# Expert down projection in three fp32r passes: low weight parts over the raw ones, four slots, empty list entries skipped

## The chip, the cores and the metric

One core of one Trainium2 chip runs the whole kernel in one launch. The metric is device time in microseconds; lower is better. The profile comes from one execution, which is a different one from the timed runs.

## The reference, cut to what matters

One decoder layer over 2048 prompt tokens and 64 sample tokens (2112 in all), width 1024: an input modulation, a projection into two mixers, an output projection with a layer norm, then a mixture of 32 experts and a second layer norm. The change touches the experts. What they compute:

```python
xt = u.reshape(B * L, D)                      # 2112 rows of 1024
eid = grp[:, None] * 8 + top_i                # two experts of one group for each row
def expert_block(args):                       # 128 rows of one expert
    xblk, ex = args
    h = jax.nn.silu(xblk @ w_gate[ex]) * (xblk @ w_up[ex])   # 1024 -> 256
    return h @ w_down[ex]                                    # 256 -> 1024
y = jnp.einsum("tkd,tk->td", y_slot.reshape(T, 2, D), wts)
x = layer_norm(ALPHA * x + gate2 * y)
```

All of it is float32. Each of the 32 experts has a gate, an up and a down matrix of 1 MB.

## The kernel before

The kernel runs five phases one after the other, each a block of five engine programs: `modulation_phase`, `mixer_phase`, `output_phase` (output projection, first norm, router logits, most of the routing), `expert_phase` and `combine_phase` (sum of a row's two expert results, second norm).

**Routing.** For each row the output phase and the head of the expert phase scatter two list entries into a list in memory; every expert has a region of 17 x 128 entries in it. An entry is (row of the input, row of the result, weight, 0). The list is first filled: an entry without a token reads the zero row `NTOK` of `u2_scratch` and writes one of 128 spare rows behind the results. The fill pattern is made in `output_phase`: POOL writes `slot_i` and `fill` (L1335 to L1337), DVE turns them into spare row numbers (L1500, L1502) in its turn of tile 0, and POOL sends the list after tile 1 (L1363).

**Blocks.** The expert phase works through blocks of 128 list entries, `total` of them, each expert with at least one and the total made even. PE runs `block_step(g, half)`: first half of `gate_up` of block g+1, transposes of the hidden rows of block g (L1908) and of the gathered rows of block g+2 (L1875), second half of `gate_up` (L1886, 24 matmuls of 512 columns in all, three fp32r passes over high and low parts), then the down projection of block g (L1925): four fp32 matmuls of 512 columns, which the trace shows as eight.

**Split of the weights.** `w_gate` and `w_up` land in `gu_raw`, three slots (`RAW`). ACT copies half a slot (128 x 2048) to the fp32r tile `gu_hi` (L1536, `split_high`), DVE subtracts it from the raw half into `gu_lo` (L1543, `split_low`); `gu_hi` and `gu_lo` have two slots. The down weights `dn_w` are used raw.

**Order on ACT and DVE.** Both run `expert_loop`: for each expert e the blocks before its last, `block_work(g, None)`, then `split_gu(e + 2, 0)`, the first half of the weights two experts on, then `block_work(last, e + 2)`, which has the second half inside it. For experts 30 and 31 nothing is split. ACT's `block_work(g)`: copy of the hidden transposes `hhT` (L1751), high part of block g+2 (`x_hi`, L1742), sigmoid of block g+1 (L1746), perhaps the second half split, and last the wait for the down projection of g and the copy `y_sb` with the weight (L1758). DVE's: low part `x_lo` (L1790), gate products `gsil`, `hh` (L1795, L1797), perhaps the second half split.

**Loads.** SP loads three experts ahead of everything, then in a loop `gate_up(e)`, which waits until expert e-3 is split, and `down(e - 1)`, which waits until the down projections up to expert e-4 are done. Every load waits for the landing of the one before it. POOL gathers the rows of block g+4 (L1684) and scatters the result of block g (L1718) by indirect transfers.

The order that matters below, as it stands in `expert_loop`:

```python
if gu_next is not None:
    split_gu(gu_next, 0, last)
block_work(last, gu_next)
```

Of the kernel before, what the change touches and what calls it, by code (L numbers as in the profile page):

```python
# [13 lines left out]

# [7 lines left out]
P = 128  # L22
D = 1024
KT = D // P
# [4 lines left out]
NTOK = SEQ + NSAMP  # L29
# [1117 lines left out]
def output_phase(nc, io, keep, scr):  # L1147
# [4 lines left out]
    T = TILES  # L1152
    LAST = T - 1
    with ExitStack() as ctx:
# [24 lines left out]
        slot_i = wo_raw[:, 6, 0:NLIST].bitcast(I32)  # L1179
# [16 lines left out]
        consts, fill_pre, fill_rdy, init_out, list_out = sem("consts2"), sem("fill_pre"), sem("fill_rdy"), sem("init_out"), sem("list_out")  # L1196
# [10 lines left out]
        with nc.Block() as block:  # L1207
# [108 lines left out]
            def _(pool):  # L1316
                pool.memset(u2[0:1, 1, :], 0.0)
# [14 lines left out]
                pool.wait_ge(consts, 1)  # L1332
                pool.dma_start(scr["u2"][NTOK:NTOK + 1, :], u2[0:1, 1, :]).then_inc(init_out, 16)
# [4 lines left out]
                pool.drain().then_inc(fill_pre, 1)  # L1338

                def tile(t):  # L1340
# [10 lines left out]
                    if t == 1:  # L1351
                        pool.wait_ge(init_out, 16)
# [90 lines left out]
            def _(dve):  # L1443
# [48 lines left out]
                for t in range(T):  # L1492
# [46 lines left out]
def split_low(dve, keep, e, a, s, r):  # L1539

    lo, hi = a * KT * DE, (a + 1) * KT * DE
    dve.wait_ge(keep["gu_h"], 2 * e + (a + 1))
    dve.tensor_tensor(w_slot(keep["gu_lo"], s, lo, hi), w_slot(keep["gu_raw"], r, lo, hi),  # L1543
                      w_slot(keep["gu_hi"], s, lo, hi).bitcast(F32), ALU.subtract).then_inc(keep["gu_l"], 1)
# [8 lines left out]
def expert_phase(nc, io, keep, scr):  # L1553
# [10 lines left out]
    gu_hi, gu_lo, dn_w, gu_l = keep["gu_hi"], keep["gu_lo"], keep["dn_w"], keep["gu_l"]  # L1564
# [7 lines left out]
    with ExitStack() as ctx:  # L1572
# [9 lines left out]
        hhT = sb("hhT", [P, KD, P])  # L1582
        y_sb = sb("y_sb", [P, 2, D])
# [25 lines left out]
        hT, hT_sb = sem("hT_ps"), sem("hT_sb")  # L1609
        dn, y_rdy, cur = sem("dn_done"), sem("y_rdy"), sem("cur_rdy")  # L1610
        kept = sem("kept")
# [8 lines left out]
        def expert_loop(eng, split_gu, block_work):  # L1620


            def expert(e, gu_next):
# [13 lines left out]
        with nc.Block() as block:  # L1637
            @block.sync
            def _(sp):
                def gate_up(e, s):  # L1640
                    if not (isinstance(e, int) and e < RAW):
                        wait_apart(sp, gu_l, 2 * (e - RAW) + 2, tick)
# [23 lines left out]
                gate_up(3, 0)  # L1666
                with sp.Fori(4, NE) as e:
                    gate_up(e, sp.snap(e % RAW))
                    down(e - 1, sp.snap((e - 1) % RAW))
                down(NE - 1, (NE - 1) % RAW)  # L1670

            @block.gpsimd
            def _(pool):
# [7 lines left out]
                def gather(b, at_ring, half):  # L1681
# [8 lines left out]
                pool.wait_ge(sc_out, 16 * 2 * (T - 12))  # L1690
                pool.dma_start(ids_ring[:, 0, :], scr["list"][0:P, :]).then_inc(ids_in, 16)
# [13 lines left out]
                def block(g, half):  # L1705
# [12 lines left out]
                    pool.indirect_dma_start(scr["y2"], bass.IndirectOffsetOnAxis(ap=ids_cur[:, half, 1:2], axis=0), y_sb[:, half, :], None).then_inc(y_out, 16)  # L1718
# [11 lines left out]
            def _(act):  # L1730
# [8 lines left out]

                def x_evac(b, half):  # L1740
# [584 lines left out]
```

## Time and profile before

| what | us |
|---|---|
| three runs | 1929.07, 1932.70, 1926.23 |
| median of the runs | 1929.07 |
| time of the profiled execution | 1924.06 |
| its span, first to last instruction | 1922.5 |
| first to last down projection, from the first start to the last | 1300.70 to 1793.99 |
| share of the span in which PE, DVE, ACT, POOL are busy | 91%, 60%, 32%, 30% |

The profile lists the busy time of each engine, its instructions in order of time with the idle time before them and what ended it, and a table of windows with the granted clock of TensorE (1.00 is 2.4 GHz). PEld is the weight load of PE. The timed runs lie up to 8.6 us above the profiled one, with a median 5.0 us above it.

### The profile page before, as it was taken

How to read it: one execution, taken by the hardware profiler on the slowest of the kernel's cores; microseconds unless marked ns; L12 is line 12 of the kernel's file. 1: busy time of each engine (PE TensorE's matmuls, PEld its weight loads, DVE VectorE, ACT ScalarE, POOL GpSimd, SP SyncE). 2: the span in 40 equal slices, each digit the busy share in tenths (PEclk: the TensorE clock that was granted, in tenths of full speed). 3: DMA queues.
4: the chain of work that ended last, by engine and by line, in shares of the span. 5: the costliest groups of instructions: out<-in, count | busy, mean ns of one | idle time of the engine just before them, and what ended most of it. 6: DMA issues, size and time to landing. Idle time of an engine off the chain costs nothing. (4 is left out here: it accounts for less than half of the span.)

```text
span 1922.5 us, 29621 instructions
## 1 busy us (share of the span) xinstructions
PE 1758.6 (91%) x9156; PEld 1378.1 (72%) x9157; DVE 1146.3 (60%) x1864; ACT 618.9 (32%) x770; POOL 586.1 (30%) x685
## 2 busy tenths in 40 slices
PE   5999999999999999999699999439999999999675
PEld 2888788888888899999577878326776677767321
DVE  3566655566666665666366877744466333455298
ACT  2333322233333322222131111025465434455233
POOL 0122221122222221122025466533344333334155
PEclk7999999999999999999899999659999999999897
DMA  8544344444333223332275443278899874798595
GB/s 258 151 133 123 96 140 133 118 125 138 89 105 93 84 61 89 94 101 68 71 247 193 132 132 121 93 263 284 301 353 379 299 238 167 250 322 313 202 397 177
DMA packets 301930, 342.76 MB, mean 178 GB/s; under 512 B 18932, under 2 KB 257300, under 8 KB 299391
## 3 DMA queue, kind: packets, MB, share of 16 engines
q1 hardware_dynamic: 278726, 284.30, 45.9%
q0 software_dynamic: 18000, 55.87, 7.9%
q10 hardware_dynamic: 5106, 1.31, 0.4%
q8 instruction: 57, 0.93, 0.2%
q14 instruction: 41, 0.34, 0.1%
HBM read 276.86 MB, written 64.58 MB: 178 GB/s over the span
## 5 line engine op out<-in xcount | busy, mean ns | idle before, releaser
L1543 DVE TENSOR_TENSOR w_gu_lo<-w_gu_raw,w_gu_hi (+1 forms) x64 | 146.5, 2292 | 133.3 <-ACT w_gu_hi L1536 121.8
L896 DVE TENSOR_TENSOR w_lo<-w_raw,w_hi 128x1024 fp32r<-128x1024 f32 x112 | 138.1, 1236 | 139.3 <-ACT w_hi L546 136.6
L658 POOL TENSOR_TENSOR o_r<-o_ms,neg_half 128x4 f32<-128x4 f32 (+1 forms) x16 | 16.8, 1050 | 663.1 <-DVEq L932 663.1
L713 PE MATMUL pr<-ub_hi,w_hi 128*128 128x288 f32 (+1 forms) x672 | 189.2, 335 | 0.0
L1886 PE MATMUL ph<-w_gu_hi,x_hi 128*128 (+1 forms) x408 | 183.5, 450 | 2.5 <-DVE x_lo L1790 2.5
L713 PE MATMUL pr<-ub_hi,w_lo 128*128 128x288 f32 (+1 forms) x672 | 184.2, 328 | 0.0
L713 PE MATMUL pr<-ub_lo,w_hi 128*128 128x288 f32 (+1 forms) x672 | 183.6, 327 | 0.0
L713 PE MATMUL pr<-ua_hi,w_hi 128*128 128x512 f32 x448 | 182.7, 408 | 0.0
L1925 PE MATMUL py<-w_dn_w,hhT 128*128 x400 | 179.9, 592 | 2.1 <-ACT hhT L1751 2.1
L713 PE MATMUL pr<-ua_lo,w_hi 128*128 128x512 f32 x448 | 177.0, 395 | 0.0
L713 PE MATMUL pr<-ua_hi,w_lo 128*128 128x512 f32 x448 | 177.0, 395 | 0.0
L1886 PE MATMUL ph<-w_gu_hi,x_lo 128*128 (+1 forms) x408 | 160.2, 393 | 0.0
L1886 PE MATMUL ph<-w_gu_lo,x_hi 128*128 (+1 forms) x408 | 160.0, 392 | 0.0
L546 ACT ACTIVATE w_hi<-w_raw 128x1024 fp32r<-128x1024 f32 x112 | 118.0, 1054 | 51.7 <-PE pr L713 42.5
L1790 DVE TENSOR_TENSOR x_lo<-pxe,x_hi 128x1024 f32 (+1 forms) x52 | 63.5, 1220 | 117.6 <-ACT x_hi L1742 117.6
L1536 ACT ACTIVATE w_gu_hi<-w_gu_raw (+1 forms) x64 | 121.9, 1907 | 34.1 <-DMA w_gu_raw<-in_w_e_up 18.7
L1925 PEld LDWEIGHTS py<-w_dn_w,hhT 128*128 128x128 f32 x400 | 75.5, 189 | 78.5 <-issue 74.8
L713 PEld LDWEIGHTS pr<-ub_hi,w_hi 128*128 128x128 f32 x672 | 113.3, 188 | 18.0 <-issue 9.0
L1718 POOL DMA_INDIRECT y_scratch<-y_sb,ids_cur x50 | 51.6, 1031 | 239.4 <-ACT y_sb L1758 210.2
L713 PEld LDWEIGHTS pr<-ub_hi,w_lo 128*128 128x128 f32 x672 | 113.4, 188 | 10.2
L713 PEld LDWEIGHTS pr<-ub_lo,w_hi 128*128 128x128 f32 x672 | 113.7, 188 | 8.8
L670 POOL TENSOR_TENSOR kl<-kl,wl 128x256 f32<-128x256 f32 (+1 forms) x112 | 89.0, 795 | 95.0 <-DVEq L1035 77.8
(337 smaller groups left out, 3502.1 us busy)
## 6 DMA issues: line engine op xcount, KB each, us to landing
w_raw<-in_w_in SPq DMA_DIRECT2D x112, 512.0 KB, 4.2
w_gu_raw<-in_w_e_gate SPq DMA_DIRECT2D x32, 1024.0 KB
w_gu_raw<-in_w_e_up SPq DMA_DIRECT2D x32, 1024.0 KB
w_dn_w<-in_w_e_down SPq DMA_DIRECT2D x32, 1024.0 KB
w_mod<-in_w_mod SPq DMA_DIRECT2D x16, 1024.0 KB
y_t<-y_scratch SPq DMA_DIRECT2D x16, 1024.0 KB, 7.6
w_ring<-in_w_mod SPq DMA_DIRECT2D x4, 2048.0 KB, 17.5
x_cols<-in_x_prompt SPq DMA_DIRECT2D x32, 256.0 KB, 5.4
```

Source lines behind the costliest of these rows:

```text
L546: act.activation(w_hi[:, n % WS], w_raw[:, n % WRAW], ACT.Copy).then_inc(hi_done, 1)
L658: pool.tensor_tensor(o_r[:, 0:c], o_ms[:, 0:c], keep["neg_half"][:, 0:c], ALU.pow).then_inc(o_rs, 1)
L670: pool.tensor_tensor(dst[:, :, 0, :], src[:, :, 0, :], wr, ALU.mult)
L713: last = pe.matmul(pr[n % 2][:, a * 512:a * 512 + c], w[:, n % WS, k, :], x[:, k, a * c:(a + 1) * c], start=(k == 0 and m == 0), stop=(k = ...
L896: dve.tensor_tensor(w_lo[:, n % WS], w_raw[:, n % WRAW], w_hi[:, n % WS].bitcast(F32), ALU.subtract).then_inc(lo_done, 1)
L1536: act.activation(w_slot(keep["gu_hi"], s, lo, hi), w_slot(keep["gu_raw"], r, lo, hi), ACT.Copy).then_inc(keep["gu_h"], 1)
L1543: dve.tensor_tensor(w_slot(keep["gu_lo"], s, lo, hi), w_slot(keep["gu_raw"], r, lo, hi), w_slot(keep["gu_hi"], s, lo, hi).bitcast(F32), AL ...
L1718: pool.indirect_dma_start(scr["y2"], bass.IndirectOffsetOnAxis(ap=ids_cur[:, half, 1:2], axis=0), y_sb[:, half, :], None).then_inc(y_out, 16)
L1790: dve.tensor_tensor(x_lo[:, bass.ds(half, 1), :].rearrange("p a w -> p (a w)"), px[:, :], x_hi[:, bass.ds(half, 1), :].rearrange("p a w -> ...
L1886: last = pe.matmul(ph[:, half, :], x[:, half, k * P:(k + 1) * P], w_slot(w, s, k * GU, (k + 1) * GU), start=(k == 0 and m == 0), stop=(k = ...
L1925: last = pe.matmul(py[:, hf * 512:(hf + 1) * 512], hhT[:, k, :], w_slot(dn_w, s_down, at, at + 512), start=(k == 0), stop=(k == KD - 1))
```

## The change

In the expert phase:

- The down weights are split like the others: ACT writes `dn_hi` (two slots), DVE the low part. `expert_loop` gets `split_dn(e + 1)` behind the last block of expert e, on ACT and on DVE. The hidden rows are split as well: ACT's copy becomes `hT_hi`, and DVE's `block_work` begins with the low part `hT_lo`. PE does twelve fp32r matmuls of 512 columns for a down projection, and waits for `hT_l` and `dn_l` in place of `hT_sb` and `wd_in`.
- `gu_lo` and `dn_lo` lie over the raw slots, and there are four slots instead of three. A gate and up load of expert e now waits until the gate-up matmuls of all blocks up to expert e-4 are done, where it waited for the split of e-3; `down(e)` stands directly behind `gate_up(e)`.
- `y_sb` and the small routing tiles share one tile, `board`.

In the routing: an entry without a token now holds the row number `NO_ROW` twice, which lies beyond both bounds; the gather and the scatter skip it. POOL clears `xg` once. The zero row, the spare rows, `slot_i` and DVE's two instructions on it are gone.

```diff
-RAW = 3
+RAW = 4
+NO_ROW = 2 * NTOK
@@ output_phase, POOL and DVE
-                pool.iota(slot_i[:, :], pattern=[[1, NLIST]], base=0, channel_multiplier=NLIST)
-                pool.iota(fill[:, :, 0], pattern=[[0, NLIST]], base=NTOK, channel_multiplier=0)
+                pool.iota(fill[:, :, 0:2], pattern=[[0, NLIST], [0, 2]], base=NO_ROW, channel_multiplier=0)
                 pool.memset(fill[:, :, 2:4], 0)
-                    if t == 0:
-                        dve.wait_ge(fill_pre, 1)
-                        dve.tensor_scalar(slot_i[:, :], slot_i[:, :], P - 1, None, ALU.bitwise_and)
-                        dve.drain()
-                        dve.tensor_scalar(fill[:, :, 1], slot_i[:, :], 2 * NTOK, None, ALU.add)
-                        dve.drain().then_inc(fill_rdy, 1)
@@ helpers
+def split_down_high(act, keep, e, s, r):
+    act.wait_ge(keep["wd_in"], 16 * e + 16)
+    act.activation(w_slot(keep["dn_hi"], s, 0, DE // P * D), w_slot(keep["dn_w"], r, 0, DE // P * D), ACT.Copy).then_inc(keep["dn_h"], 1)
+
+def split_down_low(dve, keep, e, s, r):
+    dve.wait_ge(keep["dn_h"], e + 1)
+    dve.tensor_tensor(w_slot(keep["dn_lo"], r, 0, DE // P * D), w_slot(keep["dn_w"], r, 0, DE // P * D), w_slot(keep["dn_hi"], s, 0, DE // P * D).bitcast(F32), ALU.subtract).then_inc(keep["dn_l"], 1)
@@ expert_loop
                 block_work(last, gu_next)
+                if not (isinstance(e, int) and e == NE - 1):
+                    split_dn(e + 1)
@@ SP
-                        wait_apart(sp, gu_l, 2 * (e - RAW) + 2, tick)
+                        wait_apart(sp, gu, blocks_before(sp, e - (RAW - 1)), tick)
@@ POOL, gather and scatter
-                                            bass.IndirectOffsetOnAxis(ap=ids_now[:, 0:1], axis=0)).then_inc(xg_in, 16)
+                                            bass.IndirectOffsetOnAxis(ap=ids_now[:, 0:1], axis=0),
+                                            bounds_check=NTOK - 1, oob_is_err=False).then_inc(xg_in, 16)
+                pool.memset(xg[:, :, :], 0.0).then_inc(cleared, 1)
@@ ACT and DVE, block_work
-                    act.activation(hhT[:, :, :], pht[:, 0:KD * P].rearrange("p (k t) -> p k t", k=KD), ACT.Copy).then_inc(hT_sb, 1)
+                    act.activation(hT_hi[:, :, :], pht[:, 0:KD * P].rearrange("p (k t) -> p k t", k=KD), ACT.Copy).then_inc(hT_h, 1)
+                    dve.wait_ge(hT_h, g + 1)
+                    dve.tensor_tensor(hT_lo[:, :, :], pht[:, 0:KD * P].rearrange("p (k t) -> p k t", k=KD),
+                                      hT_hi[:, :, :].bitcast(F32), ALU.subtract).then_inc(hT_l, 1)
                     x_evac(g + 2, dve.snap(g % 2))
@@ PE, block_step
-                    pe.wait_ge(hT_sb, g + 1)
-                    pe.wait_ge(wd_in, 16 * e_now + 16)
+                    pe.wait_ge(hT_l, g + 1)
+                    pe.wait_ge(dn_l, e_now + 1)
                     pe.wait_ge(y_rdy, g + 1)
-                            last = pe.matmul(py[:, hf * 512:(hf + 1) * 512], hhT[:, k, :], w_slot(dn_w, s_down, at, at + 512),
-                                             start=(k == 0), stop=(k == KD - 1))
+                            for m, (x, w) in enumerate(((hT_hi, hi), (hT_hi, lo), (hT_lo, hi))):
+                                last = pe.matmul(py[:, hf * 512:(hf + 1) * 512], x[:, k, :], w,
+                                                 start=(k == 0 and m == 0), stop=(k == KD - 1 and m == 2))
```

## Rows read from the trace of the kernel before

**Rows 1.** The page, part 1: busy us (share of the span) and instructions.

```profile
PE 1758.6 (91%) x9156; PEld 1378.1 (72%) x9157; DVE 1146.3 (60%) x1864; ACT 618.9 (32%) x770; POOL 586.1 (30%) x685
```

**Rows 2.** Windows (start:end, length, busy us by engine, PEclk, DMA share, GB/s), expert phase.

```profile
1300.70:1794.00 493.30, 491.22 (x2060) 346.22 (x2059) 234.52 (x208) 247.25 (x256) 186.34 (x248) 1.00 0.82 286
1400.83:1470.90 70.07, 70.07 (x295) 49.48 (x294) 45.31 (x36) 44.83 (x42) 29.99 (x35) 1.00 1.06 380
```

**Rows 3.** Timeline of PE (start, us, line, operation, count [idle before]), one block.

```profile
1400.83 3.59 PE L1925 MATMUL py<-w_dn_w,hhT 128*128 x8
1403.86 0.79 PE L1886 MATMUL ph<-w_gu_hi,x_hi 128*128 x1
1404.49 0.40 PE L1886 MATMUL ph<-w_gu_lo,x_hi 128*128 x1
1404.72 0.39 PE L1886 MATMUL ph<-w_gu_hi,x_lo 128*128 x1
...
1410.84 3.59 PE L1925 MATMUL py<-w_dn_w,hhT 128*128 x8
```

**Rows 4.** Timeline of ACT and DVE, a one-block expert.

```profile
1404.59 1.12 ACT L1758 ACTIVATE y_sb<-py,ids_cur 128x1024 f32 x1 [1.24 <-PE py L1925]
1406.74 1.91 ACT L1536 ACTIVATE w_gu_hi<-w_gu_raw  x1 [1.03 <-issue]
1409.02 2.29 DVE L1543 TENSOR_TENSOR w_gu_lo<-w_gu_raw,w_gu_hi  x1 [3.11 <-ACT w_gu_hi L1536]
1411.23 1.22 DVE L1790 TENSOR_TENSOR x_lo<-pxe,x_hi 128x1024 f32 x1
...
1412.36 0.41 DVE L1795 TENSOR_TENSOR gsil<-ph,gsig 128x256 f32<-128x256 f32 x1
```

**Rows 5.** Timeline of ACT, a last block behind another of its expert.

```profile
1334.51 1.12 ACT L1758 ACTIVATE y_sb<-py,ids_cur 128x1024 f32 x1 [3.05 <-PE py L1925]
1335.52 1.90 ACT L1536 ACTIVATE w_gu_hi<-w_gu_raw  x1
```

**Rows 6.** Timeline of ACT: first splits of one-block experts, first and last of 19.

```profile
1316.65 1.92 ACT L1536 ACTIVATE w_gu_hi<-w_gu_raw  x1 [1.05 <-issue]
...
1759.83 1.91 ACT L1536 ACTIVATE w_gu_hi<-w_gu_raw  x1 [1.01 <-DMA w_gu_raw<-in_w_e_up]
```

**Rows 7.** Timeline of ACT and PE where the hidden rows came late.

```profile
1481.42 0.36 ACT L1751 ACTIVATE hhT<-pht 128x256 f32<-128x256 f32 x1
...
1482.18 3.69 PE L1925 MATMUL py<-w_dn_w,hhT 128*128 x8 [1.08 <-ACT hhT L1751]
```

**Rows 8.** Timeline, output phase, tiles 0 and 1.

```profile
993.92 2.99 DVE L1447 TENSOR_TENSOR y_lo<-y_raw,y_hi 128x1024 fp32r<-128x1024 f32 x1 [0.57 <-ACT y_hi L1270]
...
997.00 2.46 DVE L1500 TENSOR_SCALAR wo_raw<-wo_raw 128x561 int32<-128x561 int32 x1
...
1000.36 1.23 DVE L1459 TENSOR_TENSOR z<-pm,mod_p 128x1024 f32<-128x1024 f32 x1
...
1014.51 1.97 PE L1390 MATMUL px<-ident,u 128*128 128x128 f32 x8 [3.78 <-POOL u L1357]
```

**Rows 9.** Timeline of PE, combine phase: two tiles behind a wait.

```profile
1847.72 5.37 PE L2054 MATMUL ps_y<-y_t,ident 128*128 128x512 f32 x8 [1.98 <-DVE zw L2063]
...
1859.43 3.67 PE L2054 MATMUL ps_y<-y_t,ident 128*128 128x512 f32 x8 [2.38 <-DVE zw L2063]
```

**Rows 10.** Windows (columns of Rows 2), the first of these tiles.

```profile
1847.70:1852.70 5.00, 4.98 (x8) 2.02 (x8) 4.70 (x8) 1.58 (x3) 2.44 (x4) 0.66 1.02 420
```

**Rows 11.** Timeline of POOL, start of the expert phase.

```profile
1283.72 1.00 POOL L1684 DMA_INDIRECT xg<-u_scratch,ids_now  x1 [0.80 <-POOL ids_now L1682]
...
1288.05 0.19 POOL L1682 COPY ids_now<-ids_ring 128x4 int32<-128x4 int32 x1 [2.23 <-DMA xg<-u_scratch,ids_now]
```

**Rows 12.** Timeline, end of the expert phase.

```profile
1799.85 1.01 POOL L1718 DMA_INDIRECT y_scratch<-y_sb,ids_cur  x1 [5.88 <-ACT y_sb L1758]
...
1807.85 0.35 SPq L1975 DMA_DIRECT2D y_t<-y_scratch  x1
```

More of the change, by code:

```diff
@@ L1563, in expert_phase @@
     ident, blk_tab, exp_tab = keep["ident"], keep["blk_tab"], keep["exp_tab"]
-    gu_hi, gu_lo, dn_w, gu_l = keep["gu_hi"], keep["gu_lo"], keep["dn_w"], keep["gu_l"]
+    gu_hi, gu_lo, dn_hi, dn_lo, gu_l, dn_l = (keep[n] for n in ("gu_hi", "gu_lo", "dn_hi", "dn_lo", "gu_l", "dn_l"))
     wg_in, wu_in, wd_in = keep["wg_in"], keep["wu_in"], keep["wd_in"]
@@ L1581, in expert_phase @@
         hh = sb("hh", [P, DE])
-        hhT = sb("hhT", [P, KD, P])
-        y_sb = sb("y_sb", [P, 2, D])
+        hT_hi = sb("hT_hi", [P, KD, P], F32R)
+        hT_lo = sb("hT_lo", [P, KD, P], F32R)
+        y_sb = R["board"][:, :].rearrange("p (a d) -> p a d", a=2)
         ids_ring = sb("ids_ring", [P, RING, 4], I32)
@@ L1618, in blocks_before, with expert_loop @@
             return eng.value_load(exp_tab[0:1, bass.ds(e, 1)], min_val=0, max_val=MAXB)
-        def expert_loop(eng, split_gu, block_work):
+        def expert_loop(eng, split_gu, split_dn, block_work):
             def expert(e, gu_next):
@@ L1665, in _ @@
                 sp.wait_ge(xg_in, 32)
[L1666 to L1670, printed above, removed]
+                with sp.Fori(RAW, NE) as e:
+                    s = sp.snap(e % RAW)
+                    gate_up(e, s)
+                    down(e, s)
             @block.gpsimd
@@ L1717, in block @@
                         wait_apart(pool, y_out, 16 * g, tick)
-                    pool.indirect_dma_start(scr["y2"], bass.IndirectOffsetOnAxis(ap=ids_cur[:, half, 1:2], axis=0), y_sb[:, half, :], None).then_inc(y_out, 16)
+                    pool.indirect_dma_start(scr["y2"], bass.IndirectOffsetOnAxis(ap=ids_cur[:, half, 1:2], axis=0), y_sb[:, half, :], None,
+                                            bounds_check=NO_ROW - 1, oob_is_err=False).then_inc(y_out, 16)
                 block(0, 0)
@@ L1738, in split_gu, with split_dn @@
                     split_high(act, keep, e, a, act.snap(e % 2), act.snap(e % RAW))
+                def split_dn(e):
+                    split_down_high(act, keep, e, act.snap(e % 2), act.snap(e % RAW))
                 def x_evac(b, half):
@@ L1779, in _ @@
                 act.wait_ge(tab_sb, 1)
-                expert_loop(act, split_gu, block_work)
+                expert_loop(act, split_gu, split_dn, block_work)
             @block.vector
@@ L1786, in split_gu, with split_dn @@
                     split_low(dve, keep, e, a, dve.snap(e % 2), dve.snap(e % RAW))
+                def split_dn(e):
+                    split_down_low(dve, keep, e, dve.snap(e % 2), dve.snap(e % RAW))
                 def x_evac(b, half):
@@ L1862, in _ @@
                 dve.wait_ge(tab_sb, 1)
-                expert_loop(dve, split_gu, block_work)
+                expert_loop(dve, split_gu, split_dn, block_work)
             @block.tensor
@@ L1884, in gate_up @@
                             pe.wait_ge(gu_l, 2 * e + 2)
-                        for m, (x, w) in enumerate(((x_hi, gu_hi), (x_hi, gu_lo), (x_lo, gu_hi))):
-                            last = pe.matmul(ph[:, half, :], x[:, half, k * P:(k + 1) * P], w_slot(w, s, k * GU, (k + 1) * GU),
+                        hi = w_slot(gu_hi, s, k * GU, (k + 1) * GU)
+                        lo = w_slot(gu_lo, r, k * GU, (k + 1) * GU)
+                        for m, (x, w) in enumerate(((x_hi, hi), (x_hi, lo), (x_lo, hi))):
+                            last = pe.matmul(ph[:, half, :], x[:, half, k * P:(k + 1) * P], w,
                                              start=(k == 0 and m == 0), stop=(k == KT - 1 and m == 2))
@@ L1900, in _ @@
                 transposes(0, 0)
-                gate_up(0, 0, 0, 0, lambda: transposes(1, 1))
+                gate_up(0, 0, 0, 0, 0, lambda: transposes(1, 1))
                 pe.wait_ge(tab_sb, 1)
@@ L1917, in between @@
                         transposes(g + 2, half)
-                    gate_up(g + 1, e_next, s_next, 1 - half, between)
-                    pe.wait_ge(hT_sb, g + 1)
-                    pe.wait_ge(wd_in, 16 * e_now + 16)
+                    gate_up(g + 1, e_next, s_next, r_next, 1 - half, between)
+                    pe.wait_ge(hT_l, g + 1)
+                    pe.wait_ge(dn_l, e_now + 1)
                     pe.wait_ge(y_rdy, g + 1)
@@ L2300, in build, with weights @@
         with ExitStack() as ectx:
-            for name, slots, width, dt in (("gu_raw", RAW, 2 * KT * DE, F32), ("gu_hi", 2, 2 * KT * DE, F32R),
-                                           ("gu_lo", 2, 2 * KT * DE, F32R), ("dn_w", RAW, DE // P * D, F32)):
-                keep[name] = ectx.enter_context(nc.sbuf_tensor("w_" + name, [P, slots, width], dt))
-            for name in ("wg_in", "wu_in", "wd_in", "gu_h", "gu_l"):
+            def weights(stack, name, slots, width, dt):
+                keep[name] = stack.enter_context(nc.sbuf_tensor("w_" + name, [P, slots, width], dt))
+            GUW, DNW = 2 * KT * DE, DE // P * D
+            with ExitStack() as landing:
+                weights(landing, "gu_raw", RAW, GUW, F32)
+                weights(landing, "dn_w", RAW, DNW, F32)
+            weights(ectx, "gu_lo", RAW, GUW, F32R)
+            weights(ectx, "dn_lo", RAW, DNW, F32R)
+            weights(ectx, "gu_hi", 2, GUW, F32R)
+            weights(ectx, "dn_hi", 2, DNW, F32R)
+            for name in ("wg_in", "wu_in", "wd_in", "gu_h", "gu_l", "dn_h", "dn_l"):
                 keep[name] = ectx.enter_context(nc.semaphore(name))
```

67 lines of the change are left out of this document (39 added, 28 removed).

## Prediction

> **What bounds the kernel now.** I read the page's busy times first: PE is busy in 91% of the span, and DVE, the engine that gets most of the new work, in 60% [rows 1]. These shares are means over five phases, so I cut the expert phase out with the windows. From the first to the last down projection it is 493.3 us, PE is busy in 491.2 of them at a granted clock of 1.00, DVE in 234.5, ACT in 247.3 [rows 2]. The timeline of PE shows a block: the eight fp32 records of one down projection start at 1400.83, those of the next at 1410.84, with no idle time between: 10.01 us a block, and 49 of these make 490.5 [rows 3]. The 2.8 us left over lie in two or three waits in the middle. So PE bounds all 50 blocks, and less PE work pays as long as nobody else is late. The rest of the argument is whether somebody becomes late.
>
> **PE, per block.** The down projection takes from 1400.83 to 1403.86, and the first fp32r matmul behind it needs 0.63 where the ones after it follow at 0.23 [rows 3]. I take both together: 3.66 us from the start of the fp32 records to the second fp32r matmul. With the change these are 13 fp32r matmuls of 512 columns. Their pace is 0.228 us (23 of them and the transposes fill 1404.49 to 1410.84 [rows 3]), so 2.96 us. PE wins 0.70 us a block: 10.01 becomes **9.31 us**, if nothing else is late. Over 49 steps that is 34 us.
>
> **ACT and DVE: the new ring.** Added are one copy of 128 x 2048 on ACT and one subtraction of that size on DVE for each expert, and one subtraction of 128 x 256 on DVE for each block. Their durations have rows: 1.91 and 2.29 us (the halves of gate and up have the same size), and 0.41 us for a 128 x 256 operation from PSUM [rows 4]. In sum DVE gets 32 x 2.29 + 50 x 0.41 = 94 us on top of 234.5, and stays under 70% of the stretch. By busy time it fits. By order it need not: `split_dn(e + 1)` stands behind ACT's wait for the down projection of the last block of e; `split_gu(e + 3, 0)` of the next expert stands behind that; and on DVE the new `hT_lo`, for which PE now waits, stands behind both of their low parts. When expert e+1 has only one block, all this lies between two down projections. I add it up, from the start of one down projection (0):
>
> - `y_sb` starts when the matmuls are done. The last of twelve starts at 2.51 and takes 0.39; `y_sb` started 0.17 behind the end of the old ones (1400.83 + 3.59 to 1404.59) [rows 3, 4], so 3.07, and 3.12 because a first record behind a wait is up to 0.1 longer (3.69 for 3.59) [rows 3, 7].
> - `split_dn` on ACT follows `y_sb` at 1.01 after its start, as the split does in a two-block expert [rows 5]: 4.13 to 6.04.
> - The low part on DVE starts some 0.3 later (0.37 from 1408.65 to 1409.02) [rows 4]: 6.34.
> - The low part of `split_gu` comes right behind it. Its high part on ACT is done by 6.04 + 1.91 = 7.95, before DVE is free, so it costs nothing; two subtractions follow each other at 2.21 (1409.02 to 1411.23) [rows 4]: 8.55, and `hT_lo` starts at 10.76 and ends at 11.17.
> - PE starts 0.40 behind the operation it waits for (1481.78 to 1482.18) [rows 7]: **11.6 us**.
>
> That is 1.6 us more than the 10.01 of now, and PE, done in 9.3, waits 2.3 us in each. What hides behind what: ACT's control work between `y_sb` and the next split shows now as 1.03 us of idle time behind a `y_sb` of 1.12 [rows 4]. I price it at nothing, because 1.9 us of new ACT work covers it; if that fails, the first split ends at 8.98 instead of 7.95 and the ring takes 12.4 us.
>
> The Trainium skill bears on this ("Advanced Engine Details and Errata", Sequencer and Instruction Queues): the sequencer goes on reading while its engine works, and ACT and DVE have queues of eight. By that rule the control work is covered and the ring takes 11.6; without it, 12.4. No row here shows ACT with two long operations queued before a loop's end, so the run will tell.
>
> **Where an expert has more blocks.** Before its first block only the down split is in the way: 6.34 + 2.21 + 0.41 + 0.40 = 9.36. Before its last block only `split_gu` is: 3.12 + 1.01 [rows 5] + 1.91 + 0.37 + 2.21 + 0.41 + 0.40 = 9.43. Blocks between these have neither. So these steps stay near PE's 9.31; I take 9.36.
>
> **How many of each.** In the timeline the first split of a one-block expert comes 1.0 us behind the end of `y_sb`, that of a longer one with it. I count 19 one-block experts with this pattern [rows 6] and 11 longer ones; the two last experts have no split of gate and up. The steps are then 19 x 11.6 + 30 x 9.36 = 220.4 + 280.8 = 501.2 us against 493.3: **+7.9 us**. The gain of PE (30 x 0.65 = 19.5, and the 2.8 of waits) is less than what the ring takes (19 x 1.6 = 30.2).
>
> **The clock.** A wait of 2.3 us is new to this stretch, whose clock is 1.00 throughout [rows 2]. The combine phase has waits of this size on PE: of eight tiles behind waits of 1.96 to 2.38 us five took 5.37 us or more, and three took 3.67, with the same instructions [rows 9]; the granted clock of such a slow tile is 0.66 over 5 us, so it was at 1.2 GHz at first and rose to 2.4 [rows 10]. A fall costs 1.7 us, and the down projection that starts behind the wait is on the ring. Bounds: no fall, 0; a fall at each, 19 x 1.7 = 32. The expert phase works more densely than the combine phase, but the wait is as long, so I take half: **+16 us**.
>
> **Loads.** The loads for expert e now start when the gate-up of e-4 is done, some two steps before they are needed (23 us and more), and 3 MB take 8.3 us at the 380 GB/s of seven one-block steps, where DMA was full (share 1.06) [rows 2]. With steps of 11.6 us and the empty entries not moved, the demand falls from 380 to below 340 GB/s. I price them at 0; if they came late, each one-block step could lose 1.3, as the two late ones of now did.
>
> **At the start** the fourth expert's 3 MB are on the way when POOL gathers blocks 0 to 2. The gather of block 1 takes 4.3 us now [rows 11]; with weights beside it I allow 6 to 8, so between 0 and +4, and some of it has slack: **+1.6**. The added split of expert 0 and POOL's clearing of `xg` (128 x 2048) lie in idle time of DVE, ACT and POOL ahead of the first gather.
>
> **Output phase.** DVE's two instructions on the fill pattern stand between `y_lo` and the next tile's `z`: 996.91 to 1000.36. Without them everything behind `z` moves 3.3 us, up to the transposes for which PE waits 3.78 us [rows 8]. Behind them PE is busy nearly throughout, so it is kept: **-3.3**. POOL's longer fill is in its idle time.
>
> **At the end** the last scatter is issued at 1799.85, and the combine phase begins 8 us later [rows 12]. If most entries of the last block are empty, up to 3 us go: **-1**. Elsewhere skipped entries shorten only transfers that nobody waits for: 0.
>
> **Sum:** +7.9 + 16 + 1.6 - 3.3 - 1 = +21. The profiled execution would go from 1924.06 to 1945. The median of the runs lies 5.0 above the profiled one, so I add 21 to 1929.07: **1950 us**. A difference of 0.3% (5.8 us) is about what a measurement can tell from none.
>
> **Rivals.**
>
> 1. *The ring without the clock.* The clock stays at 1.00, as it does at the two waits of 1.0 to 1.1 us in this phase [rows 7]. Then +21 - 16 = +5: 1934. Against it: the waits are twice as long, and [rows 9]. Chance 0.2.
> 2. *The ring, longer.* Falls at nearly each wait, or control work that is not covered (19 x 0.8 = 15): +21 + 16 to + 31, around 1970 and up to 1981. Chance 0.17.
> 3. *PE bounds as before* (the other side). It needs DVE ready within 9.3 us in the one-block steps: that the two low parts (4.4 us) don't both lie between `y_sb` and `hT_lo`, say because ACT gets ahead of the down projection it waits for. Then 49 x 9.31 = 456.2, so -37, and with start, end and output phase -40: 1889. It decides from a ring of 9.3; for any gain at all the ring must stay under 10.9. Speaking for it: the busy sums alone (DVE 234.5 + 94 = 329, ACT 247.3 + 32 x 1.9 = 308, of 456). Against: the order of the two programs, each in order. Chance 0.13. The Trainium skill ("FP8 and Floating Point Precision", TensorE Precision Notes) says that true fp32 takes four passes through the array; three for four is the gain that this case would cash in full.
> 4. *Loads come late.* The gate of the loads is one expert later than it was, and DMA was full. All 19 one-block steps lose 1.3 more: +21 + 25, 1975. Chance 0.07.
>
> The forecast itself (ring, clock falls at a part of the waits, 1935 to 1966) has 0.43.
>
> **How the numbers follow.** Faster: rival 3, 0.13, and 0.01 for rival 1 with a larger gain in the output phase: 0.14. Within 0.3% (1923.3 to 1934.9): two thirds or more of rival 1 and the low end of the forecast: 0.18. Slower: 0.68. The range reaches from 1929, rival 1 with no cost at the start, to 1981, the end of rival 2; it leaves out rival 3 and little above.
>
> **What would show it.** Right: in the timeline of a one-block expert, down projections 11.6 us apart, with PE idle 2.3 us before each and DVE (`hT_lo`) named as what ended it; on DVE `dn_lo`, `gu_lo` and `hT_lo` back to back; 9.3 to 9.4 us elsewhere; the windows of one-block stretches with a clock between 0.8 and 1.0. Wrong: steps of 9.3 throughout (rival 3); PE waiting for ACT's first split (12.4); ACT waiting for DMA (rival 4); and `z` of tile 1 no earlier behind `y_lo`.

## The result, and the profile after

| | before | changed kernel |
|---|---|---|
| median of the runs, us | 1930.88 (4 runs) | 1987.93 (4 runs, 1984.39 to 1991.03) |
| ratio to before, 95% interval | | 1.0311 (1.0288 to 1.0334) |
| profiled execution, us (its span) | 1924.06 (1922.5) | 1990.59 (1987.7) |
| first to last down projection, us | 493.3 | 560.56 (1297.92 to 1858.48) |
| 19 steps at one-block experts, mean us | 10.14 | 13.84 |
| the 30 other steps, mean us | 10.02 | 9.92 |
| first start of `z` in tile 0 to that in tile 1, output phase | 14.50 | 11.12 |

PE is TensorE, DVE VectorE, ACT ScalarE and POOL GpSimd. A step is the time from the start of one down projection to the start of the next; a one-block step is one in which ACT and DVE do all the splits of a one-block expert's turn between the two. The change makes the kernel 3.1% slower. Between the first and the last down projection 67.3 us come in, and the span grows by 65.2, so the loss lies there. The one-block steps take 262.9 us in sum where they took 192.8 (+70.1); the others give back 2.8.

The page of the changed kernel, part 1 (as [rows 1]): PE is busy in 89%, where it was in 91%, and its busy time grew from 1758.6 although it has less to do.

```profile
PE 1767.3 (89%) x9356; PEld 1437.1 (72%) x9357; DVE 1238.0 (62%) x1944; ACT 674.6 (34%) x802; POOL 627.4 (32%) x683
```

Windows of it (columns of [rows 2]): ten one-block experts, then longer ones, then seven one-block experts.

```profile
1400.00:1540.00 140.00, 111.12 (x453) 88.06 (x452) 89.73 (x71) 79.79 (x70) 55.69 (x50) 0.86 0.82 272
1540.00:1700.00 160.00, 158.23 (x766) 129.47 (x765) 74.15 (x80) 75.91 (x81) 61.60 (x81) 0.99 0.57 187
1700.00:1810.00 110.00, 95.19 (x419) 76.08 (x418) 69.71 (x58) 64.53 (x60) 46.20 (x48) 0.92 0.74 243
```

In the first window PE idles 29 of 140 us at a granted clock of 0.86. In the middle one it is nearly as full as before. DMA moves 272 GB/s where the first seven of these experts took 380 before [rows 2].

The timeline of PE, one step (answers to [rows 3]):

```profile
1407.82 0.49 PE L1945 MATMUL py<-w_dn_hi,hT_hi 128*128 x1 [1.94 <-DVE hT_lo L1812]
...
1408.60 0.47 PE L1945 MATMUL py<-w_dn_hi,hT_hi 128*128 x1
1408.87 0.63 PE L1945 MATMUL py<-w_dn_lo,hT_hi 128*128 x1
...
1411.86 0.56 PE L1945 MATMUL py<-w_dn_hi,hT_lo 128*128 x1
1412.25 0.40 PE L1903 MATMUL ph<-w_gu_hi,x_hi 128*128 x1
...
1422.47 0.79 PE L1945 MATMUL py<-w_dn_hi,hT_hi 128*128 x1 [3.43 <-DVE hT_lo L1812]
```

And ACT and DVE in the same step (answers to [rows 4]):

```profile
1412.59 1.12 ACT L1765 ACTIVATE board<-py,ids_cur 128x1024 f32 x1 [4.36 <-PE py L1945]
1413.60 1.90 ACT L1537 ACTIVATE w_dn_hi<-w_dn_w  x1
1415.41 1.90 ACT L1525 ACTIVATE w_gu_hi<-w_gu_raw  x1
...
1415.84 2.29 DVE L1542 TENSOR_TENSOR w_dn_lo<-w_dn_w,w_dn_hi  x1 [4.14 <-ACT w_dn_hi L1537]
1419.46 2.29 DVE L1532 TENSOR_TENSOR w_gu_lo<-w_gu_raw,w_gu_hi  x1 [1.33 <-issue]
1421.67 0.42 DVE L1812 TENSOR_TENSOR hT_lo<-pht,hT_hi 128x256 fp32r<-128x256 f32 x1
```

Read together, these are the ring: down projection 1407.82, `y_sb` (now a part of `board`) 4.77 later, `dn_lo` 3.25 after that, `gu_lo` 3.62 after that, `hT_lo` 2.21 after that, the next down projection 0.80 later. In sum 14.65. The parts in their order are the predicted ones, and two have another size. `y_sb` comes late because eight of the twelve matmuls run at half the pace (0.43 us apart, 1.2 GHz) before PE is back at 0.23. The windows of this step show the clock: it is still 1.00 in the wait, and 0.50 from one microsecond behind the start of the burst.

```profile
1405.50:1407.80 2.30, 0.37 (x2) 0.00 (x0) 2.30 (x3) 1.75 (x2) 2.30 (x1) 1.00 1.05 363
1408.80:1412.20 3.40, 3.40 (x9) 2.64 (x8) 2.72 (x3) 0.00 (x0) 0.00 (x0) 0.50 0.65 218
```

And `gu_lo` doesn't follow `dn_lo` at once: DVE idles 1.33 us "<-issue", waiting for nothing that the profile shows.

The waits from 1290 to 1870 and, in the second fence, the page's group of the first matmul of each three: nearly all of PE's idle time is `hT_lo`. The third line is DVE's gap, once in each one-block step; the fourth is ACT's wait for POOL's copy of the slot numbers, which holds `y_sb` back in three blocks.

```profile
ACT board L1765 <- PE py L1945: 153.7, 47, 7.1
PE py L1945 <- DVE hT_lo L1812: 54.4, 20, 3.9
DVE w_gu_lo L1532 <- issue: 13.5, 19, 1.8
ACT board L1765 <- POOL ids_cur L1716: 8.2, 3, 2.7
```

```profile
L1945 PE MATMUL py<-w_dn_hi,hT_hi 128*128 x200 | 94.0, 470 | 55.2 <-DVE hT_lo L1812 54.4 <-issue 0.5
```

ACT has no wait for DMA in this stretch, so the loads are not late. In the output phase the gap that DVE's two fill instructions left is closed (answers to [rows 8]):

```profile
984.50 1.22 DVE L1454 TENSOR_TENSOR z<-pm,mod_p 128x1024 f32<-128x1024 f32 x1
...
992.45 3.08 DVE L1442 TENSOR_TENSOR y_lo<-y_raw,y_hi 128x1024 fp32r<-128x1024 f32 x1 [0.48 <-ACT y_hi L1271]
995.62 1.22 DVE L1454 TENSOR_TENSOR z<-pm,mod_p 128x1024 f32<-128x1024 f32 x1
...
1009.56 1.97 PE L1385 MATMUL px<-ident,u 128*128 128x128 f32 x8 [3.35 <-POOL u L1352]
```

### The profile page after: what moved, and what is told of

The parts are those of the page before. It is cut to its first block and busy times, and to the rows that moved or that the text cites. A ratio compares the mean times of both kernels' runs of the same rounds, so it can differ in the third digit from the quotient of the medians.

```text
span 1987.7 us, 30591 instructions
## 1 busy us (share of the span) xinstructions
PE 1767.3 (89%) x9356; PEld 1437.1 (72%) x9357; DVE 1238.0 (62%) x1944; ACT 674.6 (34%) x802; POOL 627.4 (32%) x683
## 5 line engine op out<-in xcount | busy, mean ns | idle before, releaser
L660 POOL TENSOR_TENSOR o_r<-o_ms,neg_half 128x4 f32<-128x4 f32 (+1 forms) x16 | 16.8, 1051 | 662.9 <-DVEq L934 662.9
L1903 PE MATMUL ph<-w_gu_hi,x_hi 128*128 (+1 forms) x408 | 167.4, 410 | 5.8 <-issue 3.4
L1945 PE MATMUL py<-w_dn_hi,hT_hi 128*128 x200 | 94.0, 470 | 55.2 <-DVE hT_lo L1812 54.4
L1542 DVE TENSOR_TENSOR w_dn_lo<-w_dn_w,w_dn_hi (+1 forms) x32 | 73.4, 2292 | 103.9 <-ACT w_dn_hi L1537 103.9
L1721 POOL DMA_INDIRECT y_scratch<-board,ids_cur x50 | 51.4, 1028 | 266.2 <-issue 261.6
L1765 ACT ACTIVATE board<-py,ids_cur 128x1024 f32 x50 | 55.9, 1117 | 161.9 <-PE py L1945 153.7
## 6 DMA issues: line engine op xcount, KB each, us to landing
w_gu_raw<-in_w_e_up SPq DMA_DIRECT2D x32, 1024.0 KB, 10.5
```

Source lines behind the costliest of these rows:

```text
L1542: dve.tensor_tensor(w_slot(keep["dn_lo"], r, 0, DE // P * D), w_slot(keep["dn_w"], r, 0, DE // P * D), w_slot(keep["dn_hi"], s, 0, DE // P ...
L1765: act.activation(y_sb[:, bass.ds(now, 1), :].rearrange("p a d -> p (a d)"), py[:, :], ACT.Copy, scale=ids_cur[:, bass.ds(now, 1), 2:3].rea ...
L1903: last = pe.matmul(ph[:, half, :], x[:, half, k * P:(k + 1) * P], w, start=(k == 0 and m == 0), stop=(k == KT - 1 and m == 2))
L1945: last = pe.matmul(py[:, hf * 512:(hf + 1) * 512], x[:, k, :], w, start=(k == 0 and m == 0), stop=(k == KD - 1 and m == 2))
```

## The experiments

Ten kernels ran. Each ratio is to runs of the kernel before taken beside it. "Falls" are the down projections behind the one-block steps, of 19, that ran partly at 1.2 GHz by the granted clock.

### One place of the ring at a time

**`hT_lo` first.** On DVE the first half of the next gate and up split goes behind `hT_lo` in the last block's work:

```diff
-                if gu_next is not None:
+                if gu_next is not None and not low_first:
                     split_gu(gu_next, 0, last)
@@ DVE, block_work, behind hT_lo
+                    if gu_next is not None:
+                        split_gu(gu_next, 0)
```

> The changed kernel with one thing moved: on DVE, in the last block of an expert, hT_lo comes ahead of the first low part of gate and up, no longer behind it. Nothing is left out. Theory (a ring of y_sb, split_dn on ACT, low part of down, low part of gate and up, hT_lo, down projection; PE then waits some 2.3 to 3 us and its clock falls): 2.2 us leave the ring of each of the 19 one-block steps, and with the wait under 1 us the clock stays up. These steps then take 9.8 to 10.4 us instead of 13.8, the whole some 65 to 75 us less than the changed kernel: 1915 to 1925. Rival a (twelve fp32r matmuls and their weight tiles are slow by themselves, or memory placement is): steps stay above 12, 1970 or more. Rival b (the loads come too late with the new gate): no change either, since the order on DVE doesn't touch loads: 1980 to 1990.

Measured: 1922.51, ratio 0.9966 (0.9951 to 0.9981); 495.5 us from first to last down projection, one-block steps 10.73, others 9.72. With `gu_lo` and the gap ahead of it no longer between `y_sb` and `hT_lo`, 65 us are gone. The one-block step is still above PE's 9.31 and above the 9.8 to 10.4 expected, and the clock did not stay up throughout: in five of these steps PE waits 2.35 to 2.64 us, and behind four of them the clock fell. What is left shows in the waits of the same stretch:

```profile
ACT board L1765 <- POOL ids_cur L1716: 30.0, 13, 3.7
PE py L1947 <- DVE hT_lo L1812: 16.0, 8, 2.6
```

ACT's `y_sb` now waits for POOL's copy of the slot numbers in 13 blocks, where the changed kernel had three such waits (8.2 us). Here POOL's copy and ACT behind it:

```profile
1423.27 2.36 POOL L1716 COPY ids_cur<-ids_ring 128x4 int32 x1
...
1434.86 0.20 POOL L1716 COPY ids_cur<-ids_ring 128x4 int32 x1
```

```profile
1425.85 1.12 ACT L1765 ACTIVATE board<-py,ids_cur 128x1024 f32 x1 [3.38 <-POOL ids_cur L1716]
```

**Down split early.** On ACT and DVE `split_dn(e + 1)` moves into the last block's work, on ACT ahead of the wait for the down projection:

```diff
-                block_work(last, gu_next)
-                if not (isinstance(e, int) and e == NE - 1):
-                    split_dn(e + 1)
+                block_work(last, gu_next, None if isinstance(e, int) and e == NE - 1 else e + 1)
@@ ACT and DVE, block_work, behind the second half of split_gu
+                    if dn_next is not None:
+                        split_dn(dn_next)
```

> The changed kernel with split_dn(e + 1) moved, on ACT and on DVE, into the last block of expert e, ahead of ACT's wait for the down projection. Nothing is left out. Theory of the ring: the down split leaves it; what stays is y_sb at 3.1, 2.15 of control, 1.9 high part, 0.4, 2.2 low part, 0.4 hT_lo, 0.4 = 10.6 us for a one-block step, PE waits some 1.3 us, and the clock falls rarely: 1925 to 1945. Rival a (slow down projection): above 1970. Rival b (loads): the down weights are needed some 2 us earlier, so waits for DMA appear on ACT: 1990 or more.

Measured: 1917.60, ratio 0.9948 (0.9929 to 0.9966); 487.9 us, one-block steps 10.62, others 9.54. The step is what the parts give with the down split taken out (10.6 expected); the time lies below the 1925 to 1945 that was expected. PE still waits for `hT_lo` at 20 places, 0.5 to 1.1 us each, and the window of the one-block experts has the full clock:

```profile
PE py L1947 <- DVE hT_lo L1812: 15.1, 20, 1.1
```

```profile
1400.00:1540.00 140.00, 131.69 (x631) 105.97 (x630) 100.37 (x87) 92.05 (x85) 66.16 (x70) 1.00 0.88 303
```

**Both moves** together, the two diffs above:

> Both moves of the two runs before in one kernel. Theory of the ring: the chain from y_sb to hT_lo no longer has a low part in it (3.1 + 2.15 + 1.9 + 0.4 + 0.4 + 0.4 = 8.4 us), so PE bounds at 9.3 us or ACT at 9.5; 49 x 9.5 = 466 us against 493 before: 1900, faster than both kernels by 1% or more. If loads or the down projection itself cost the time, it stays above 1960.

Measured: 1903.38, ratio 0.9882 (0.9859 to 0.9904); 469.2 us, one-block steps 9.92, others 9.36. Of the 49 steps 36 now take the 9.31 that PE needs. So PE's gain is real where the ring leaves it, and the order on ACT and DVE had hidden it.

### The rest of the change alone

The down projection stays fp32, without the split of `w_dn` and `hT_lo`; slots, waits of the loads, skipped entries and the fill are the change's:

```diff
-                    pe.wait_ge(hT_l, g + 1)
-                    pe.wait_ge(dn_l, e_now + 1)
+                    pe.wait_ge(hT_h, g + 1)
+                    pe.wait_ge(wd_in, 16 * e_now + 16)
```

> The changed kernel with the down projection taken back to four fp32 matmuls on raw weights: no down split, no hT_lo. Four slots, low parts over raw ones, the new gate of the loads, skipped entries and the shared tile stay. Theory of the ring: the chain is as before the change, y_sb, split, hidden copy, under 9 us, so PE bounds at 10.0: the kernel before less what the output phase gains, 1922 to 1930. If the four slots, the gate of the loads or the skipped entries cost the time, it stays above 1960.

Measured: 1923.44, ratio 0.9980 (0.9965 to 0.9995); 495.3 us, 10.22 and 10.04 a step. Less than 0.3% and no loss: all of the 3.1% belongs to the three passes and what feeds them.

**The fill alone**, in the kernel before: DVE's two instructions are gone, and all entries without a token write one spare row.

```diff
-                pool.iota(slot_i[:, :], pattern=[[1, NLIST]], base=0, channel_multiplier=NLIST)
+                pool.iota(fill[:, :, 1], pattern=[[0, NLIST]], base=2 * NTOK, channel_multiplier=0)
```

> The kernel before with one edit in the output phase: the spare row of an entry without a token is a constant that POOL writes, and DVE's two instructions on it are gone. Nothing is left out of the result; all such entries write one spare row. Theory: z of tile 1 starts 3.3 us earlier and this is kept, 1.5 to 4 us less than the kernel before. Rival: other work is late next and takes it up, 0 to 1 us; or writes to one row are slow and cost time at the end of the expert phase.

Measured: 1930.55, ratio 1.0010 (0.9991 to 1.0029). `z` to `z` went from 14.50 to 11.16, as in the changed kernel, but the total is unmoved: the 1.5 to 4 us expected did not come. In this profile the 16th to the 19th step took 11.1 to 13.0, where the splits came late because of late loads, and first to last down projection was 498.9. So the 3.3 us are shown where they arise, and whether they reach the end is not.

### The clock

Spare 128-column fp32 matmuls ahead of PE's wait for `hT_lo` in each block of the changed kernel keep PE occupied in a part of that wait; their result goes nowhere. Eight of them, then four:

```diff
+                    for _ in range(8):
+                        pe.matmul(rk[:, 0:P], keep["ones"][:, :], keep["tri"][:, :], start=True, stop=True)
                     pe.wait_ge(hT_l, g + 1)
```

> The changed kernel with eight added 128-column fp32 matmuls on PE ahead of its wait for hT_lo in every block, into a free bank that nobody reads (1.7 us of work). Nothing is left out. Theory of the clock: in one-block steps they fit into a wait of 2.3 to 3 us, the wait that is left is about 1 us, the down projection behind it runs at 2.4 GHz, and y_sb starts 3.1 instead of 4.8 us behind its start; one-block steps go from 13.8 to 12.2 to 12.6, while the others go from 9.9 to 11.0. In sum within 10 us of the changed kernel. Rival (the slow down projections come from something else, such as weight tiles or memory placement): y_sb stays 4.8 behind, one-block steps stay at 13.8, and the whole is 30 us longer.

> The changed kernel with four spare 128-column fp32 matmuls in place of the eight of the run that kept the clock, again ahead of TensorE's wait for hT_lo in each block; their result goes nowhere. They take about 0.85 us at the full clock instead of 1.7, so that at one-block experts a wait of 1 to 3 us is left. Theory A (the falls of the clock come from TensorE's waits of 2 to 4 us): some of the 19 down projections behind the waits still run partly at 1.2 GHz, more than the 2 of 19 with eight matmuls and fewer than the 18 of 19 with none; down to y_sb at one-block experts lies between 3.2 and 4.8 on average; the other 30 steps pay 0.85 less than with eight, about 10.5; the time is 1985 to 2000. Rival B (the falls do not depend on how long TensorE waits): 15 or more of 19 still fall and the time is 2010 to 2020, the changed kernel's plus 0.6 to 0.85 for most blocks.

| | changed kernel | four | eight |
|---|---|---|---|
| median, ratio to before | 1987.93, 1.0311 | 1985.50, 1.0302 (1.0276 to 1.0327) | 2005.81, 1.0405 (1.0377 to 1.0433) |
| waits of PE in one-block steps, us | 1.9 to 3.9 | 1.3 to 2.7 | 0.2 to 2.0 |
| falls, of 19 | 18 | 5 | 2 |
| down projection to `y_sb`, mean us | 4.55 | 3.51 | 3.34 |
| one-block step, mean us | 13.84 | 12.86 | 12.83 |
| other step, mean us | 9.92 | 10.36 | 11.19 |

The first window of the three kernels has a granted clock of 0.86, 0.96 and 0.98. With eight:

```profile
1425.79 1.95 PE L1937 MATMUL rk_last<-tri,ones 128*128 128x128 f32 x16
1429.39 0.50 PE L1947 MATMUL py<-w_dn_hi,hT_hi 128*128 x1 [1.65 <-DVE hT_lo L1812]
```

PE got 0.9 (four) and 1.8 us (eight) more to do in each block, and the one-block steps still became 1.0 shorter. `y_sb` comes 1.0 and 1.2 us earlier. That is the price of the falls, and the waits cause them: shorter waits, fewer falls. With eight the one-block step (12.83 for 12.2 to 12.6) and the total (18 us above the changed kernel, for 10) missed what was expected: the 30 other steps pay 1.27 each, 38 us, where 1.1 was expected, and the one-block steps give back less than expected, because DVE's gap is no shorter (`gu_lo` 3.2 us behind `dn_lo` in the mean). With four the two sides cancel: no gain over the changed kernel.

### DVE's gap behind `dn_lo`

In the changed kernel `gu_lo` starts 2.49 to 4.06 us behind `dn_lo`, 3.00 in the mean, and 2.21 would be back to back. The lines between the two on DVE are the loop's turn to the next expert, the reading of its bounds and a branch. This run puts the low part of `w_dn` behind them, on DVE alone:

```diff
             def expert(e, gu_next):
                 first = blocks_before(eng, e)
                 last = eng.snap(eng.value_load(exp_tab[0:1, bass.ds(e + 1, 1)], min_val=1, max_val=MAXB) - 1)
+                if dn_first:
+                    split_dn(e)
@@
-                if not (isinstance(e, int) and e == NE - 1):
+                if not dn_first and not (isinstance(e, int) and e == NE - 1):
                     split_dn(e + 1)
@@ DVE, ahead of the loop
-                split_down_low(dve, keep, 0, 0, 0)
 ...
-                expert_loop(dve, split_gu, split_dn, block_work)
+                expert_loop(dve, split_gu, split_dn, block_work, dn_first=True)
```

> The changed kernel with one edit on VectorE alone: it reads the bounds of the next expert before it takes the low part of w_dn, so that this reading no longer stands between the ends of dn_lo and the start of gu_lo; what is computed is the same. In the changed kernel the start of gu_lo lies 2.98 us (mean) behind the start of dn_lo, of which 2.29 is dn_lo itself. Theory A (the gap of some 0.7 is VectorE's own reading of bounds, which the prediction priced at nothing): dn_lo to gu_lo falls to 2.2 to 2.5, the reading goes into VectorE's wait for ScalarE's w_dn_hi, the steps at one-block experts become 0.5 to 0.7 shorter (13.84 to 13.2), and the time falls by 10 to 13 us to about 1975 to 1978. Rival B (the gap is the rest of the loop's control, or the clash with GpSimd's copies): dn_lo to gu_lo stays at 2.8 to 3.0 and the time within 3 us of the changed kernel's 1988.

Measured: 1956.66, ratio 1.0162 (1.0140 to 1.0185); 520.35 us, one-block steps 11.91, others 9.80. DVE in one step:

```profile
1415.70 2.29 DVE L1542 TENSOR_TENSOR w_dn_lo<-w_dn_w,w_dn_hi  x1 [2.57 <-ACT w_dn_hi L1537]
1417.91 2.28 DVE L1532 TENSOR_TENSOR w_gu_lo<-w_gu_raw,w_gu_hi  x1
1420.11 0.42 DVE L1814 TENSOR_TENSOR hT_lo<-pht,hT_hi 128x256 fp32r<-128x256 f32 x1
```

and PE, the end of this step and that of a later one:

```profile
1420.94 0.51 PE L1946 MATMUL py<-w_dn_hi,hT_hi 128*128 x1 [2.08 <-DVE hT_lo L1814]
...
1491.08 0.79 PE L1946 MATMUL py<-w_dn_hi,hT_hi 128*128 x1 [2.06 <-DVE hT_lo L1814]
1491.67 0.63 PE L1946 MATMUL py<-w_dn_lo,hT_hi 128*128 x1
```

The gap is gone in all 19 (2.20 to 2.21), and sixteen of these steps take 11.56 to 11.73: the ring of 11.6 that was predicted. The gain is more than twice the expected one. The waits shrank to between 1.55 and 2.11 us in 18 of 19, and falls to 5, three of them in a row from the step that ends at 1491.08. So the sum for one-block steps is -36.5 us: 19 x 0.79 = 15.0 for the gap, and 19 x (4.55 - 3.41) = 21.7 for falls that no longer happen. The loop's turn and the reading of the bounds were moved as one; which of the two weighs more isn't told apart, nor why the gap varies between 0.2 and 1.8. The branch still stands between `dn_lo` and `gu_lo` here, and leaves no gap.

### The better versions

POOL's copy of the slot numbers at the top of its block's work, ahead of the list load and the gather:

```diff
+                    pool.tensor_copy(ids_cur[:, half, :], place(ids_ring, g % RING)).then_inc(cur, 1)
 ...
-                    pool.tensor_copy(ids_cur[:, half, :], place(ids_ring, g % RING)).then_inc(cur, 1)
```

With `hT_lo` first:

> The changed kernel with hT_lo ahead of the low part of the next expert's first gate and up weights on VectorE, as in the run at 1922.5, and GpSimd's copy of the slot numbers moved to the top of its block's work; the same is computed. In the run at 1922.5 ScalarE's y_sb waited 13 times on GpSimd's copy, 30.0 us in all, and the clock fell behind some of TensorE's waits. Theory A (those waits carry what is left above the run with both moves): one-block steps go from 10.73 to 9.9 to 10.2 and the time to 1903 to 1912. Rival B (the waits on GpSimd stand beside a wait for the split of w_dn that ends as late): the time stays at 1918 to 1923.

Measured: 1906.86, ratio 0.9897 (0.9877 to 0.9917); one-block steps 10.05 against 10.73, others 9.57. The waits of `y_sb` on POOL are gone, and with them every wait of PE above 1.4 us and every fall of the clock. With both moves:

> The kernel with both moves, and on POOL the copy ids_cur of block g at the top of its block, ahead of the fetch and the gather, no longer behind them. Nothing is left out. In the kernel with both moves some one-block steps still take 10 to 11 us, and there y_sb waits for that copy (2.4 us long beside DVE's work, 0.2 otherwise). Theory: y_sb then starts with the end of the down projection or of ACT's split, the steps of 10.0 to 11.0 fall to 9.3 to 9.6, 8 to 11 us less than with both moves alone. Rival: these steps come from ACT's or DVE's own control work; then nothing changes.

Measured: **1898.90, ratio 0.9852** (0.9821 to 0.9883), the fastest of all; 466.8 us, 9.80 and 9.35 a step. That is 4.5 us less than with both moves alone, where 8 to 11 were expected, and the two intervals overlap, so this last gain is not clear of noise. Its slow steps (10.5 to 11.2, from 1435 to 1490) now wait for weights, as the waits of that window show:

```profile
ACT w_gu_hi L1525 <- DMA w_gu_raw<-in_w_e_up: 14.3, 5, 3.2
```

## Why the prediction was right in its sign and wrong in its size

The forecast was 1950 with a range of 1929 to 1981; it came out at 1988. Against the sum of the prediction, in the profiled execution (+65.2 of span where +21 was summed):

| term | predicted | measured |
|---|---|---|
| ring without falls, 19 steps | 19 x 11.6 | 19 x 12.4 (the DVE gap, 0.79 each): **+15** |
| falls of the clock in it | 16 | 19 x (4.55 - 3.12) = 27.2, less the 1.7 of the next line, nearly all in the 14 one-block steps that begin with a fall: **+9.5** |
| `y_sb` held back by POOL's copy | 0 | 4.83 - 3.12 in the first one-block step, whose clock did not fall: **+1.7** |
| 30 other steps | 30 x 9.36 | 30 x 9.92: **+17** |
| down projection of the first block | +1.6 | 60.79 us from the start of the phase, against 59.70: +1.1 |
| output phase | -3.3 | `z` to `z` -3.4, and 2.5 of it is left at the expert phase's first load (3.9 earlier, of which 1.4 were there before tile 0): +0.8 |
| end | -1 | 129.2 us from the last down projection to the end, against 128.5: +0.7 |

1. **PE per block, 9.31: right.** Undisturbed steps take 9.30 to 9.34 in the changed kernel, and with both moves 36 of the 49 do.
2. **The ring's places and sizes: right but for one.** `y_sb` to `dn_lo` took 3.26 (3.22 summed), `gu_lo` to `hT_lo` 2.21, `hT_lo` to the down projection 0.80 (0.81 summed). The order on ACT and DVE is what costs, as the two moves show by taking it out one place at a time.
3. **The step that failed** is the sentence "The low part of `split_gu` comes right behind it". I had looked for control work on ACT, priced it there (0.8 us if not covered), and found none in the result: `gu_hi` follows `dn_hi` at 1.81 with no idle time. On DVE the same loop's turn stands between `dn_lo` and `gu_lo`, and I gave it no term. The subtraction's 2.29 us don't cover it. On ACT two operations cover the turn, `y_sb` and `dn_hi`: 2.82 us from the start of the first to `gu_hi`, against the 2.15 that the turn takes there. So the reading ahead on which the prediction relied hid all of it on ACT and only a part on DVE. The row that could have told stood in [rows 4]: ACT takes 2.15 us from the start of `y_sb` to its next split over the same lines of code, nearly as long as the 2.29 of cover on DVE. The Trainium skill ("Advanced Engine Details and Errata", Clock Domains) gives DVE's sequencer 0.96 GHz and the others 1.2; by that the 2.15 us would be an estimated 2.7 on DVE. Measured are 2.49 to 4.06 with a mean of 3.00, so the rule points the right way and explains neither end.
4. **The clock: right in kind, mis-sized.** "I take half" of 19 became 18. Of the 18, 14 lie at the start of one-block steps and 4 at the start of others (point 5). The half came from a combine phase whose waits were 1.96 to 2.38 us [rows 9], and there the last of the eight tiles counted has half the rows, so that it was four of seven with the same instructions; with the DVE gap the waits here grew to between 1.9 and 3.9. Where the ring had its predicted length, and the waits 1.55 to 2.11 but for one of 2.94, 5 of 19 fell: less than half. So this error is mostly a consequence of the one before. A fall does not make the wait behind it longer, since PE's own work grows with it: in the run without DVE's gap the waits behind two fallen projections were 2.07 and 2.11 us, where the others but one lie between 1.55 and 2.11.
5. **The other steps: mis-sized.** 9.36 held for the fastest; the mean was 9.92. Of the 17 us, 8.2 lie in four steps that begin with a fall (12.28, 11.06, 11.23, 11.06), and 2.4 in one of 11.81 whose clock stayed up: there ACT waited 2.74 us for POOL's copy and `y_sb` came at 5.27. I had let falls end with the one-block step, but the last one of a group falls on the first down projection of the next expert. The rest is mostly steps of 9.9 to 10.0 that alternate with 9.3; with both moves, where `hT_lo` comes earlier, all but two are gone. I read them as PE's own turn of its loop, which it can't read ahead when it reaches the wait for `hT_lo` only just in time; that reading is argued, not tested.
6. The errors add up to nearly what came out: 21.2 + 15.0 + 9.5 + 1.7 (POOL) + 16.8 + 0.8 (output phase) - 0.5 (start) + 1.7 (end) - 1.4 (by which the changed kernel's profile was ahead at tile 0 already) = 64.8, of 65.2. **Loads, start, output phase: right,** and small. No wait for a load stands in this stretch of the changed kernel; such waits came in versions with shorter steps, at 9.3 us and, with the fp32 down projection, at 10.0 (PE waits 2.8 us in sum for down weights). **End: wrong** by 1.7.

The rivals: the second (falls at nearly each wait, or control work) names falls and control work, with an "or" where the chip had "and". But its control work stood on ACT, where it was covered; that its 15 us met the 15.0 of DVE's gap is luck. Its end of 1981 is what both together give, and the other steps lie above it. The third, PE as the bound, is what the two moves restore. Its limit for any gain, a ring under 10.9, doesn't follow from the prediction's own sums: (493.3 - 280.8) / 19 is 11.2.

Had the DVE gap not been there, the forecast would have stood, in part by luck: the run without it is at a ratio of 1.0162, which is 1960 on the scale of the 1929.07. In its profile the 19 one-block steps with their falls take 226 us where 236 were summed, and the 30 others 294 where 281 were, so two misses of 10 and 13 us nearly cancel.

## What to carry to other kernels

Write the ring between two uses of the bounding engine as a list of starts, and put every loop turn and register read on every engine of it in as a term, also behind a wait, which did not absorb it here (DVE idled 4.14 us ahead of `dn_lo` and 1.33 behind it). When the ring comes out above the bounding engine's own work, the wait it makes can cost TensorE its clock, so price the ring and the falls together: 0.79 us taken out of this ring was worth 1.9 us a step. A precision trick that moves work from the busiest engine to idle ones pays (1.5% here) only after the new work is taken off the path behind the last result: split weights ahead of the wait, and serve the small operand first.

## What the runs showed of the hardware

- The granted clock falls at waits of about 2 us: 18 of 19 at waits of 1.9 to 3.9 us, 5 of 19 at 1.55 to 2.9, 5 of 19 at 1.3 to 2.7 (four spare matmuls), none at 0.5 to 1.1 (down split early). In the changed kernel the stretch at 1.2 GHz begins between 1.7 us before the burst behind the wait and 1.3 us behind the burst's start, so the first matmuls often still run at full pace. A fall costs one down projection 1.3 to 2.5 us. Equal waits differ: in the run without DVE's gap ten steps in a row ended in waits of 1.56 to 2.11 us (1409.25 to 1517.59), seven had no fall behind them and the last three had.
- POOL's copy of 128x4 takes 0.20 us or 1.3 to 2.2, and its issue of a gather 1.04 or 2.5 to 3.0, in the same loop of the changed kernel. Where the one is long the other is short, and DVE's long subtractions run beside them:

```profile
1405.35 2.66 POOL L1684 DMA_INDIRECT xg<-u_scratch,ids_now  x1 [0.86 <-POOL ids_now L1682]
1408.01 0.21 POOL L1716 COPY ids_cur<-ids_ring 128x4 int32 x1
...
1419.04 1.04 POOL L1684 DMA_INDIRECT xg<-u_scratch,ids_now  x1 [0.86 <-POOL ids_now L1682]
1420.07 1.73 POOL L1716 COPY ids_cur<-ids_ring 128x4 int32 x1
```

  DVE's `gu_lo` lay at 1404.81 to 1407.10 and at 1419.46 to 1421.75, and each long POOL instruction ends within a microsecond of it. That a small copy on POOL can wait 2 us for DVE's tile is how it looks; no run had POOL and DVE apart to show it.
